# The 64-row tile projected first in plain single precision, and the last expert slot reordered

## The reference, cut to what matters

```python
h = rmsnorm(x, norm_mix);  y = gelu(S5 state space of h @ w_in)       # 512 wide
a = y @ w_out;             x = x + a[..., :D] * sigmoid(a[..., D:])   # 512 -> 2048
logits = rmsnorm(x, norm_ffn) @ [w_rg | w_re]                         # 4 groups, 16 experts
combine = top 1 group, top 2 of its 4 experts, weights normalised
h = silu(xn @ w_gate[e]) * (xn @ w_up[e]) * combine[e]                # 1024 -> 256, per chosen expert
x = x + sum_e h @ w_down[e];  out = rmsnorm(x, norm_final)
```

## Time and profile before

| | us |
|---|---|
| median of 3 runs (860.26 to 862.54) | 860.39 |
| profiled execution | 861.41 |
| its span | 859.7 |
| TensorE busy in the span | 787.8 (92%) |
| VectorE, ScalarE, GpSimd busy | 596.9, 414.2, 330.4 |

### The profile page before, as it was taken

The page is one execution under the profiler, slowest core; times in us unless marked ns, Lnnn a source line. Parts: engine busy times, 40 slices in busy tenths (PEclk is TensorE's granted clock), DMA queues, the critical chain, the costliest instruction groups (busy, mean ns, idle before and its releaser), DMA issues.

```text
span 859.7 us, 15054 instructions
## 1 busy us (share of the span) xinstructions
PE 787.8 (92%) x4246; PEld 623.8 (73%) x4246; DVE 596.9 (69%) x1126; ACT 414.2 (48%) x772; POOL 330.4 (38%) x409
## 2 busy tenths in 40 slices
PE   6999989989999999989618999999999999999981
PEld 4788866557778778777416788888888888888871
DVE  7997889996334355363664688787866878876852
ACT  7556751125235344243303467475654656655631
POOL 3910011020000000601523467766776767766532
PEclk9999999999999999999858999999999999999996
DMA  9464316899443243332217768855867768876821
GB/s 319 148 228 149 122 32 228 188 158 298 160 148 135 86 146 124 99 113 97 74 38 275 239 199 281 278 191 211 300 192 270 248 231 278 299 254 207 291 93 76
DMA packets 57014, 161.26 MB, mean 188 GB/s; under 512 B 21520, under 2 KB 26000, under 8 KB 50256
## 3 DMA queue, kind: packets, MB, share of 16 engines
q1 hardware_dynamic: 33648, 112.99, 40.5%
q0 software_dynamic: 22976, 47.05, 15.7%
q10 hardware_dynamic: 288, 0.03, 0.0%
HBM read 129.06 MB, written 62.40 MB: 223 GB/s over the span
## 4 chain that ended last, share of the span: by engine, by line
PE 46%; DMA 3%; issue 3%; DVE 2%; POOL 1%; ACT 0%; DVEq 0%; POOLq 0%; SPq 0%; ACTq 0%
PE pbig L1259 8%; PE pbig L1255 8%; PE pbig L1256 8%; PE pbig L1280 4%; PE pbig L1282 4%; PE pbig L1281 4%; PE pbig L1243 4%; DMA WR<-in_w_gu 1%; PE pbig L1155 1%; PE pbig L1157 1%; PE pbig L1156 1%; POOL records L515 1%; PE pbig L1267 1%; DMA xg<-x_mid,recs 1%; DMA low<-records 0%
## 5 line engine op out<-in xcount | busy, mean ns | idle before, releaser
L1255 PE MATMUL pbig<-WH,xgH 128*128 x320 | 130.2, 407 | 1.6 <-ACT xgH L896 1.5
L1256 PE MATMUL pbig<-WL,xgH 128*128 x320 | 125.8, 393 | 0.0
L515 POOL DMA_INDIRECT records<-rec,at_rec x34 | 34.4, 1012 | 216.7 <-DVEq L1734 207.6
L1155 PE MATMUL pbig<-w2H,ysH 128*128 128x512 f32 (+1 forms) x272 | 112.9, 415 | 2.7 <-DVE ysL L1591 2.3
L1156 PE MATMUL pbig<-w2L,ysH 128*128 128x512 f32 (+1 forms) x272 | 108.0, 397 | 0.0
L1157 PE MATMUL pbig<-w2H,ysL 128*128 128x512 f32 (+1 forms) x272 | 107.8, 396 | 0.0
L573 POOL DMA_INDIRECT x_sums<-xg,recs x36 | 78.9, 2193 | 39.9 <-DVE xg L1851 31.7
L1741 DVE SCALAR_TENSOR_TENSOR WL<-WR,gf_p,WH 128x512 f32 (+1 forms) x128 | 86.4, 747 | 6.1 <-ACT WH L860 4.0
L860 ACT ACTIVATE WH<-WR,gf_p 128x512 f32 (+1 forms) x128 | 80.6, 713 | 5.6 <-DMA WR<-in_w_gu 4.1
L1259 PE MATMUL pbig<-WH,xgL 128*128 x320 | 81.3, 395 | 0.0
L1631 DVE TENSOR_TENSOR x<-pbig,sg 128x1024 f32<-128x1024 f32 (+1 forms) x17 | 20.8, 1225 | 85.6 <-PE pbig L1157 80.4
(11 more groups left out here) (295 smaller groups left out, 1665.0 us busy)
## 6 DMA issues: line engine op xcount, KB each, us to landing
WR<-in_w_gu SPq DMA_DIRECT2D x32, 1024.0 KB
WR<-in_w_dn SPq DMA_DIRECT2D x16, 1024.0 KB
xT<-in_x_cols SPq DMA_DIRECT2D x16, 512.0 KB, 3.7
low<-in_x_rows SPq DMA_DIRECT2D x16, 512.0 KB, 4.4
U<-in_x_rows SPq DMA_DIRECT2D x16, 512.0 KB, 5.0
x_mid<-x SPq DMA_DIRECT2D x16, 512.0 KB
x_sums<-x SPq DMA_DIRECT2D x16, 512.0 KB
w<-in_w_out SPq DMA_DIRECT2D x1, 4096.0 KB, 13.6
```

The lines of the kernel that those rows point to most:

```text
L1155: pe.matmul(pbig[0:rows, n, :], ysH[b][:, k, 0:rows], w2H[n][:, k, :], start=(k == 0), stop=False)
L1255: pe.matmul(pbig[:, 6, :], xgH[b][:, k, :], WH[:, w], start=(k == 0), stop=False)
L1256: pe.matmul(pbig[:, 6, :], xgH[b][:, k, :], WL[:, w], start=False, stop=False)
```

## The change

The tiles are numbered anew: s = 0 is the tile of 64 rows, s = 1 to 16 are the full tiles (f = s - 1). The half tile is projected by `c_half` from y and w_out as they are, without splits: for each block of k and each of two banks, two matmuls, one for each half of the 1024 columns, into partitions 0 to 63 and 64 to 127. From there on it is handled as 128 x 512; its row sums of squares are added over the two halves by a matmul with a table `pair`. TensorE's order at the start is: three blocks of k of the half tile, three of the first full tile, the fourth of each. The splits of y for f = 0 and 1 stand ahead of the loop, those of f + 2 follow in its turn. SP waits for the half tile's matmuls before it overwrites w_out with expert weights, and loads and stores the half tile in two pieces each. The record tables give tile 0 the last 64 tokens.

In the last slot, TensorE turns h first; its down product goes by halves to banks 4 and 5, VectorE sums each half there, ScalarE squares each half from there, GpSimd adds the two and takes the root, and the last norm reads the sum from PSUM. Silu and e_h have moved behind the branch. GpSimd's drain waits for older scatters before the last three, and for the last four, counted in `os_end`, at its end.

```diff
+            def c_load(s):
+                b = s % 2
+                if s >= 2:
+                    sp.wait_ge(S["x2_done"], s - 1)
+                if s == 0:
+                    for p, c in half_rows:
+                        sp.dma_start(xr[0][p, 0:512], x_rows[TF * P:NT, c]).then_inc(S["xr_in0"], 16)
+                else:
+                    sp.dma_start(xr[b], x_rows[(s - 1) * P:s * P, :]).then_inc(S[f"xr_in{b}"], 16)
+
+            def c_store(s):
+                b = s % 2
+                sp.wait_ge(S["x2_done"], s + 1)
                 for xD in (x2D, sumD):
+                    if s == 0:
+                        for p, c in half_rows:
+                            sp.dma_start(xD[TF * P:NT, c], x2[0][p, 0:512]).then_inc(S["x2_st0"], 16)
+                    else:
+                        sp.dma_start(xD[(s - 1) * P:s * P, :], x2[b][:, :]).then_inc(S[f"x2_st{b}"], 16)
...
             sp.wait_ge(S["w2_lo"], CB)
             sp.wait_ge(S["w2_hi"], CB)
+            sp.wait_ge(S["a_done"], 2)
             for c in range(CUTS):
...
+            def root_last(t):
+
+                b = t % 2
+                pool.wait_ge(S["half_sq"], 1)
+                pool.tensor_scalar(mean_half[:, :], ess_half[:, 0:1], 1.0 / D, EPS, ALU.mult, ALU.add).then_inc(S["half_mean"], 1)
+                pool.wait_ge(S["half_mean"], 1)
+                pool.wait_ge(S["half_sq"], 2)
+                pool.wait_ge(S["fo_done_e"], t - 1)
+                pool.tensor_tensor(emean[:, b:b + 1], mean_half[:, :], ess_half[:, 1:2], ALU.add).then_inc(S["mean_set"], 1)
+                pool.wait_ge(S["mean_set"], t + 1)
+                pool.tensor_tensor(eroot[:, b:b + 1], emean[:, b:b + 1], power[:, :], ALU.pow).then_inc(S["root_set"], 1)
...
             def drain(s, n):
 
-                for k in range(s, n + 3):
-                    if k < n:
-                        sum_gather(k)
+                for k in range(s, n):
+                    sum_gather(k)
                     if k - 2 < n - 4:
                         sum_scatter(k - 2)
-                    if k == n + 1:
-                        root(k - 2)
-                    if k - 3 < n:
-                        out_scatter(k - 3)
-                    if k - 2 < n - 1:
-                        root(k - 2)
-                for t in range(n - 4, n):
+                    out_scatter(k - 3, "os_end" if k - 3 >= n - 4 else None)
+                    root(k - 2)
+                for t in range(n - 8, n - 4):
                     pool.wait_ge(S[f"os{t % 4}"], 16 * (t // 4 + 1))
+                out_scatter(n - 3, "os_end")
+                root(n - 2)
+                root_last(n - 1)
+                out_scatter(n - 2, "os_end")
+                out_scatter(n - 1, "os_end")
...
+            def c_gate(s):
+
+                if s == 0:
+                    act.wait_ge(S["a_done"], 1)
+                    act.activation(sg[:, 0:512], pbig[:, 4, :], ACT.Sigmoid).then_inc(S["sig_done"], 1)
+                    return
+                act.wait_ge(S["x2_done"], s)
+                act.wait_ge(S["ssq_done"], s)
                 for n in range(2):
+                    act.wait_ge(S["a_done"], 4 * s - 1 + n)
+                    act.activation(sg[:, n * 512:(n + 1) * 512], pbig[:, 2 + n, :], ACT.Sigmoid).then_inc(S["sig_done"], 1)
+
+            def c_square(s):
+
+                b, n = s % 2, D if s else 512
+                act.wait_ge(S["x2_done"], s + 1)
+                act.activation(sg[:, 0:n], x2[b][:, 0:n], ACT.Square, accum_out=ssq[:, s:s + 1]).then_inc(S["ssq_done"], 1)
...
+            def c_turned(s):
+                if s == 0:
+                    act.wait_ge(S["xt_done"], 2)
+                    act.activation(xnT[:, 0:4, :], pbig[:, 7, :].rearrange("p (a m) -> p a m", a=4), ACT.Copy).then_inc(S["xt_evac"], 2)
+                    return
...
+            for s in range(TT):
+                c_gate(s)
+                if s >= 1:
+                    c_turned(s - 1)
+                    c_parts(s - 1)
+                if s - 1 in ROUTE_A:
+                    exps(ROUTE_A.index(s - 1))
+                if s >= 1:
+                    c_routed(s - 1)
+                c_square(s)
+                if 1 <= s < TF - 1:
                     for part in range(2):
-                        c_y_hi(t + 2, part)
+                        c_y_hi(s + 1, part)
...
+            def e_square_half(n):
+
+                act.wait_ge(S["half_sum"], n + 1)
+                act.activation(pbig[:, 2 + n, :], pbig[:, 4 + n, :], ACT.Square, scale=1.0 if n == 0 else 2.0 ** -5,
+                               accum_out=ess_half[:, n:n + 1]).then_inc(S["half_sq"], 1)
+
             def e_last(s, before):
 
                 b = s % 2
+                e_silu(s, b)
+                e_cut(s - 1, *before, (2,))
                 e_square(s - 2, b, (s - 2) % RING)
                 e_ht_hi(s, b)
-                e_cut(s - 1, *before, (2,))
                 e_square(s - 1, 1 - b, (s - 1) % RING)
-                e_square(s, b, s % RING)
+                act.wait_ge(S["acc_sq"], s)
+                for n in range(2):
+                    e_square_half(n)
...
+            def c_half(ks):
+
+                if ks[0] == 0:
+                    pe.wait_ge(S["wout_in"], 16)
+                    pe.wait_ge(S["y_in"], 16 * (CB - 1) * 8)
+                    pe.wait_ge(S["gelu_done"], G - 2)
+                for bank, n in ((4, 2), (5, 0)):
+                    for k in ks:
+                        if k == CB - 1:
+                            pe.wait_ge(S["y_tail"], 16 * 8)
+                        y = yflat[:, k, TF * P:NT] if k < CB - 1 else ylast[:, TF * P:NT]
+                        for h in range(2):
+                            mm = pe.matmul(pbig[h * ST:(h + 1) * ST, bank, :], y, w2[:, k, (n + h) * 512:(n + h + 1) * 512],
+                                           start=(k == 0), stop=(k == CB - 1))
+                    if k == CB - 1:
+                        mm.then_inc(S["a_done"], 1)
...
+            def c_turn(s):
+                b = s % 2
+                pe.wait_ge(S["x2_done"], s + 1)
+                if s == 0:
+                    pe.wait_ge(S["gelu_done"], G)
+                    for k in range(4):
+                        mm = pe.transpose(pbig[:, 7, k * P:(k + 1) * P], x2[0][:, k * P:(k + 1) * P], ident[:, :])
+                    mm.then_inc(S["xt_done"], 2)
+                    return
...
+            def c_half_sum():
+
+                pe.wait_ge(S["fold_set"], 2)
+                pe.wait_ge(S["ssq_done"], 1)
+                pe.matmul(pbig[:, 5, 0:1], pair[:, :], ssq[:, 0:1], start=True, stop=True).then_inc(S["half_ss"], 1)
...
+                    x = xnT[:, k, :] if s else xnT[:, k % 4, k // 4 * ST:(k // 4 + 1) * ST]
+                    mm = pe.matmul(pbig[c:c + 32, 6, 0:rows], wr_sb[:, k, :], x, start=(k < 4), stop=(k >= 4))
...
-            for t in range(TT):
-                if t == 0:
-                    c_proj(0, (2, 3, 0, 1), range(CB - 1))
-                    c_proj(0, (2, 3, 0, 1), (CB - 1,))
-                    pe.wait_ge(S["gelu_done"], G)
-                    continue
-                c_proj(t, (2, 3))
-                if t >= 1:
-                    c_turn(t - 1)
-                c_proj(t, (0,))
-                if t == 1:
+            blocks = (2, 3, 0, 1)
+            c_half(range(CB - 1))
+            c_proj(1, blocks, range(CB - 1))
+            c_half((CB - 1,))
+            c_proj(1, blocks, (CB - 1,))
+            c_turn(0)
+            c_half_sum()
+            for s in range(2, TT):
+                c_proj(s, (2,))
+                if s == 2:
                     pe.wait_ge(S["wr_scaled"], KD)
-                if t >= 1:
-                    c_logit(t - 1)
-                if t == TF:
+                    c_logit(0)
+                c_proj(s, (3,))
+                if s == 2:
+                    c_fold(0)
+                c_turn(s - 1)
+                c_proj(s, (0,))
+                c_logit(s - 1)
+                if s == TF:
                     positions(2)
-                c_proj(t, (1,))
-                if t >= 1:
-                    c_fold(t - 1)
-                if t in POS_AT:
-                    positions(POS_AT.index(t))
+                c_proj(s, (1,))
+                c_fold(s - 1)
+                if s in POS_AT:
+                    positions(POS_AT.index(s))
...
+            def down_half(n, out, b, off):
+                for k in range(2):
+                    w = ds(off + (KD * 2 * DE + k * D + n * 512), 512)
+                    pe.matmul(out, hTH[b][:, k, :], WH[:, w], start=(k == 0), stop=False)
+                    pe.matmul(out, hTH[b][:, k, :], WL[:, w], start=False, stop=False)
+                    mm = pe.matmul(out, hTL[b][:, k, :], WH[:, w], start=False, stop=(k == 1))
+                return mm
...
+            def e_down_last(s, b, off, e):
+                pe.wait_ge(S["ht_evac"], s + 1)
```

(46 more changed lines are left out.)

217 lines of the change are left out of this document (87 added, 130 removed).

## The result

The changed kernel takes **848.08 us** (median of 4 runs, 846.1 to 851.6). The kernel before, run beside it on the same chip, took 860.7 us (4 runs, 860.26 to 862.54). The ratio is 0.9854, 95% interval 0.9817 to 0.9891, so 12.6 us less. The forecast was 9.8 less, 850.6. The profiled execution of the changed kernel took 848.98 us, with a span of 847.2 us against 859.7.

The account below looks back on a forecast made before the run. TensorE was taken as the bound, busy 92% of the span, with only latency counting in the two chains. Terms -8.1 + 1.1 + 0.5 - 3.3 = -9.8 us gave 850.6 us; 8-in-10 range 847 to 857.

Parts of the forecast that it names:

- Front, -8.1: Start of the projections: cheaper half-tile matmuls and an earlier start at full clock save 8.1 us.
- 3.0 later end, 11.0 for the removed matmuls: Projection start: front ends 3.0 us later but holds both tiles, while the last tile's 48 matmuls, 11.0 us, leave.
- pace of 0.213 us a record: Half tile on TensorE: each 512-column record takes 0.213 us, 32 records 6.8 us, with two column halves overlapping.
- The slower pair of the earlier trace: Line 993 in the old trace: two records at half pace, read as the engine going from low to full clock.
- loads stand exposed: Rival for the half tile: each of 32 records pays about 0.14 us of weight load; +4.4 us, 855.0, 4%.
- The halves run in turn: Rival for the half tile: column halves do not overlap, 13.7 us in place of 6.8; 857.4 us, 6%.
- A new wait, +1.1: Second logit in the projections: TensorE waits for xnT behind ScalarE's steps, once, +1.1 us, bounds 0 and 2.
- the slower rival: Rival in the projections: the 1.1 us wait repeats in all 15 full tiles, 15.4 us more, 866.0; 4%.
- The bridge, +0.5: Small steps between projections and experts: ending with a full tile makes xnT and copy lt longer, +0.5 us.
- The end, -3.3: Last slot: h turned first, no idle before down(s), sums and squares in halves; last scatter 3.3 us earlier.
- the rival: Rival for the end: silu or h come only after branches, or GpSimd's order holds the scatter; +3.3, 853.9, 12%.
- the same point in time as before: nothing: Kernel end: GpSimd's wait for the last four scatters, moved to its very end, changes nothing.

Follow-up runs that it names:

- e5: Changed kernel with the half tile's records six of one column half, then six of the other, twice: 849.59 us, ratio 0.9867 to the kernel before.
- e11: Changed kernel with twelve half-tile records of one column half, then twelve of the other: 845.49 us, a single run; kernel before 851.8 beside it.
- e10: The changed kernel run once more with no edit: 850.04 us, ratio 0.9869 to the kernel before.
- e2: Kernel before with only the new last slot and GpSimd's moved wait, old projections: 855.34 us, ratio 0.9957 to the kernel before.
- e4: Kernel before with only GpSimd's last wait moved outside the branches (with `os_end` and renamed semaphores): 857.35 us, ratio 0.9987.
- e7: Changed kernel with the last slot's silu and product h put back ahead of ScalarE's and VectorE's last branch: 849.93 us, ratio 0.9880 to the kernel before.
- e1: Changed kernel's half-tile projections with the old last slot and end: 853.9 us, ratio 0.9939 to the kernel before.
- e3: Changed kernel with GpSimd's wait for the last four scatters put back inside the drain: 851.15 us, ratio 0.9907 to the kernel before.
- e6: Changed kernel with the half tile's first matmul again waiting for the full tile's first ysL: 849.12 us, ratio 0.9876 to the kernel before.
- e9: Changed kernel plus 20 unread matmuls on TensorE ahead of the first turn of gathered rows: 851.39 us, ratio 0.9886 to the kernel before.

## Why the prediction was right, and where it was not

The direction, the mechanism and most terms held: -8.1 at the front and -3.3 at the end are by far the largest, and the runs of each alone show both. The sum was 9.8 and the spans of the two profiled executions show 12.5; the differences by terms:

- **Front, -8.1.** The step "3.0 later end, 11.0 for the removed matmuls" is met: the front's end moved by 19.67 - 16.74 = 2.93 us. The pace of 0.213 us a record, the start after the last transfer, the full clock: as said. The reason given for the pace, two halves side by side, is shown by e5 and e11; only the reading that a record of 512 columns passes once, in 0.213 us, is wrong: a record takes 0.43 us and a pair shares it. The slower pair of the earlier trace rows was put down to a low clock; the windows list 1.00 for 11.5 to 12.4 us, so no row bears that out, and nothing else hung on it. The rival "loads stand exposed" did not come: 24 records in 5.30 us leave no room for 0.14 us of load each. The rule of the Trainium skill behind it (TensorE: Matmul & The Clock Gate, packing small matmuls: a load overlaps matmuls in flight only when their row groups differ) does not hold as it stands for these column halves; the same section elsewhere excepts loads into a background weight buffer, which the forecast left out. The same section calls matmuls strictly first in, first out; the 14 and 20 steps of e5 and e11, where strict order makes 21 and 23, speak against that too. "The halves run in turn" did not come either, and e11 prices an order that goes in that direction: a whole half first costs 3.5 us in the first 24 records.
- **A new wait, +1.1: too large.** It measured 0.16. The fold ended 6.6 us after its tile's start, about as taken (6.35). But the logit, square, splits, sigmoids and copies took 3.8 us in all (218.72 to 222.56), where the forecast had 3.8 without the logit, and the logit, the way to it and gaps on top; and TensorE wanted xnT 10.3 us after the tile's start, not 9.9. It came once, and the slower rival (a wait in every tile) not at all.
- **The bridge, +0.5:** 0.2, from the last but one fold to the first turn 32.21 before and 32.41 after. The "remote" wait went from 4.19 to 3.20, within the bounds given; in e10 and e11 it is gone, so it belongs to the execution and not to the change.
- **Not in the sum: a low clock in the old kernel's projections.** Stage to first turn is 9.3 us shorter where the terms made 6.5. One us is the wait above. 1.7 us more were lost by the kernel before at a low clock near its 382nd us, in the windows of before, then of after at the same work:

```profile
380.00:382.00 2.00, 1.88 (x8) 1.59 (x9) 1.43 (x8) 0.38 (x2) 0.00 (x0) 0.77 0.00 0
382.00:384.00 2.00, 2.00 (x6) 1.59 (x5) 1.86 (x2) 0.02 (x1) 0.00 (x0) 0.50 0.00 0
384.00:386.00 2.00, 2.00 (x9) 1.58 (x9) 0.69 (x5) 1.98 (x5) 0.00 (x0) 0.87 0.61 246
```

```profile
374.00:376.00 2.00, 2.00 (x10) 1.63 (x9) 1.61 (x3) 0.38 (x2) 0.00 (x0) 1.00 0.00 0
```

  A deficit of 0.23, 0.50 and 0.13 of two us each. All three kernels with the full tile first have such a stretch between 375 and 387 us (before, e2, e4), and of the ten with the half tile first only e7 has. TensorE idles 1.6 us just ahead of it in before as in after (1.65 and 1.63), so why the clock stays up in the new order is open.
- **The end, -3.3:** 2.8. The shape is as said: h turned first, no idle before down(s), sums and squares in halves. Two sizes differ. silu behind ScalarE's branch came 0.9 later than before, where the forecast had the branch hidden in some 5 us of idle; the rival had named this place, and of the signs of being wrong this one did come (silu more than 0.3 us late). So the last matmul is 1.7 us nearer to the last up in place of 2.4. Each half's sum costs 0.76 us, not 0.64, and from the last matmul to the norm it is 0.7 us less, for 0.9. Against that stands 0.4 us that the forecast had not: the last scatter starts 2.08 us behind the norm's start, for 2.52, since in the kernel before the scatter ahead of it held GpSimd until 848.15 (timeline of the kernel before):

```profile
846.09 2.06 POOL L589 DMA_INDIRECT out_y<-fo,recs  x1 [0.19 <-issue]
```

- **GpSimd's moved wait, "the same point in time as before: nothing": this step failed.** It is worth 2.1 to 3.0 us (e4, and after against before), 2.6 from the landing of the last scatter to the end, where two instruction transfers no longer stand. The wait does end at the same moment, but the way out of the nested branches, which stood behind it, is now beside the scatters. The text had counted 3.71 us for ScalarE's branch one paragraph on and asked nothing of GpSimd's.
- **First product, +1.5, and the untouched stages, +1.2:** neither was in the sum. 13 matmuls of the first product pass at half pace for 6 before (0.2 us each more); in the others it is 0 to 13, 13 in e2 too, which has the full tile first, and 6 or 7 in e1, e3, e4, e6 and e11, so this is chance. So is the +1.2: the last group of the stage before starts between 189.1 and 192.5 us in all of them.

The account closes: 9.8 + 0.9 (the wait) + 0.3 (bridge) + 1.7 (old low clock) + 3.0 (GpSimd's way out) - 0.5 (end) - 1.5 - 1.2 = 12.5 us. So the forecast was right by mechanism, and its nearness to the result owes something to luck: 5.9 us of gain that it did not have, against 3.2 of loss. It also took 0.3% as what tells a change from none; 28 runs of the kernel before lie between 856.17 and 864.15 us.

## What to carry to other kernels

Before a kernel ends, look at what stands behind its last wait: work or branches that don't need the waited-for transfers belong ahead of the wait, where they run beside the transfers (2.6 us here). A branch is hidden only where its engine idles anyway; moving one moves its price onto whatever is next on that engine, so list that engine's next steps and who waits for them (e7: 3 us). And where TensorE is fed faster after a chain of small steps, ask first when the next weights arrive (e9).

## What the runs showed of the hardware

- Plain single-precision matmuls on 64 columns of the array: two records a matmul, each 0.43 us for 512 columns at the full clock, and one of either column half in the same time. In the counts a record of the other half passes three that wait, in e5 as in e11, not more.
- The clock after an idle is not the same from run to run. In the last slot, TensorE idled 1.99 us in the changed kernel and 2.11 in e2 and stayed at full clock, 2.14 in the second execution of the changed kernel and fell; at the start of the projections it stayed after 1.68 (e6) and was low after 2.31 (before).
- The way out of nested branches, ahead of the end: two packets of the instruction queue some 2.2 us apart, 2.6 us in all when they stand behind the last scatter's landing.
